# Two blocks on one core: the gaps of a gated scan's level move into the operands' buffer, and the modulation's transposes to another place

## The reference

```python
def hgrn_forget(z, lb):
    f = lb + (1.0 - lb) * jax.nn.sigmoid(z)
    return 1.0 - f, jnp.log(f)                      # key, log of the forget gate

def step(s, xs):                                    # gla_chunk_scan
    bcum = jnp.cumsum(fc, axis=1)
    o_inter = einsum('bthk,bhkv->bthv', qf * jnp.exp(bcum), s)
    diff = bcum[:, :, None] - bcum[:, None, :]
    decay = jnp.exp(jnp.where(incl, diff, -inf))
    att = einsum('bthk,bshk,btshk->bhts', qf, kf, decay)
    o_intra = einsum('bhts,bshv->bthv', att, vf)
    ...
```

## Time and profile before

| | |
|---|---|
| median of three runs | 1472.39 us |
| the profiled execution | 1471.23 us |
| its span | 1469.5 us |
| TensorE matmuls, busy | 1411.3 us (96%) |
| TensorE weight loads, busy | 1155.2 us (79%) |
| VectorE, busy | 563.9 us (38%) |
| ScalarE, busy | 415.0 us (28%) |
| GpSimd, busy | 157.2 us (11%) |

### The profile page before, as it was taken

The page is one execution under the profiler, slowest core; times in us unless marked ns, Lnnn a source line. Parts: engine busy times, 40 slices in busy tenths (PEclk is TensorE's granted clock), DMA queues, the critical chain, the costliest instruction groups (busy, mean ns, idle before and its releaser), DMA issues.

```text
span 1469.5 us, 20226 instructions
## 1 busy us (share of the span) xinstructions
PE 1411.3 (96%) x8130; PEld 1155.2 (79%) x8130; DVE 563.9 (38%) x1335; ACT 415.0 (28%) x771; POOL 157.2 (11%) x191
## 2 busy tenths in 40 slices
PE   5999999999999999999999999999979999999986
PEld 3888788888878888888888888877757788887765
DVE  1262322111226432313235431245664533466363
ACT  2112212412011222333323312331333422433432
POOL 0110300000011030000111100003230000142100
PEclk9999999999999999999999999999989999999998
DMA  9544544355445444443333332455313433322200
GB/s 388 218 163 152 206 172 172 134 200 194 184 164 211 175 173 172 149 179 117 141 126 132 115 127 103 144 200 201 116 58 144 172 119 147 126 112 87 87 29 29
DMA packets 31485, 221.76 MB, mean 151 GB/s; under 512 B 3872, under 2 KB 4000, under 8 KB 4896
## 3 DMA queue, kind: packets, MB, share of 16 engines
q1 hardware_dynamic: 31392, 220.47, 40.5%
HBM read 219.41 MB, written 1.05 MB: 150 GB/s over the span
## 4 chain that ended last, share of the span: by engine, by line
PE 84%; DVE 7%; ACT 2%; issue 2%; POOL 2%; DMA 1%; DVEq 0%; SPq 0%; ACTq 0%; POOLq 0%
PE event L879 43%; PE event L870 9%; PE event L1023 6%; PE event L1067 5%; PE logits L955 3%; PE mixed_out L1011 3%; PE event L836 3%; PE event L1035 2%; PE turns L974 2%; PE event L1167 2%; PE event L1094 1%; DMA ring<-in_w 1%; PE event L1048 1%; DVE logits L1612 1%; ACT S L1284 1%
## 5 line engine op out<-in xcount | busy, mean ns | idle before, releaser
L879 PE MATMUL event<-u,ring 128*128 128x256 f32 x3200 | 717.7, 383 | 15.3 <-ACT region L1233 9.5
L879 PEld LDWEIGHTS event<-u,ring 128*128 128x128 f32 x3200 | 605.7, 191 | 113.0 <-issue 30.9
L870 PE MATMUL event<-ring,u 128*128 128x256 f32 (+1 forms) x704 | 150.9, 371 | 0.0
L870 PEld LDWEIGHTS event<-ring,u 128*128 128x128 f32 x704 | 127.4, 190 | 20.9 <-issue 4.9
L1975 POOL TENSOR_TENSOR raw<-raw,tables 128x512 f32<-128x512 f32 (+1 forms) x28 | 44.7, 1595 | 758.3 <-DVE turned L1588 449.5
L1248 ACT ACTIVATE region<-event 128x512 f32<-128x512 f32 x72 | 43.0, 597 | 279.9 <-PE event L879 279.7
L1284 ACT ACTIVATE S<-logits,stat 128x512 f32<-128x512 f32 (+2 forms) x160 | 83.8, 535 | 127.8 <-DVE stat L1627 123.2
L1067 PE MATMUL event<-region,ring 128*128 128x256 f32 x384 | 85.1, 380 | 2.9 <-DVE region L1770 2.9
L1023 PE MATMUL event<-region,ring 128*128 128x256 f32 x384 | 84.4, 380 | 0.0
L1067 PEld LDWEIGHTS event<-region,ring 128*128 128x128 f32 x384 | 72.2, 190 | 15.2 <-issue 5.9
L1023 PEld LDWEIGHTS event<-region,ring 128*128 128x128 f32 x384 | 72.6, 190 | 11.1 <-issue 1.4
(11 more groups left out here) (208 smaller groups left out, 1307.5 us busy)
## 6 DMA issues: line engine op xcount, KB each, us to landing
ring<-in_w SPq DMA_DIRECT2D x204, 1024.0 KB, 4.8
tables<-in_two SPq DMA_DIRECT2D x1, 1472.0 KB, 8.0
x<-in_x SPq DMA_DIRECT2D x1, 1024.0 KB, 14.8
x<-in_ctx SPq DMA_DIRECT2D x1, 1024.0 KB, 6.7
out<-x SPq DMA_DIRECT2D x4, 256.0 KB, 2.2
tables<-in_one SPq DMA_DIRECT2D x1, 768.0 KB, 9.9
tables<-in_late SPq DMA_DIRECT2D x1, 512.0 KB, 5.6
consts<-in_common SPq DMA_DIRECT2D x1, 320.0 KB, 3.3
```

The lines of the kernel that those rows point to most:

```text
L870: ins = mm(bank[:, t * 256:t * 256 + width], mem.u[:, q, k, t * P:(t + 1) * P], wt[:, k * 256:k * 256 + width], start=k == 0, stop=k == KB ...
L879: ins = mm(bank[:, j * 256:(j + 1) * 256], wt[:, k * 256 + j * P:k * 256 + j * P + P], mem.u[:, q, k, :], start=k == 0, stop=k == KB - 1)
```

## The change

Two edits. In the first, GpSimd writes the gaps of prep p straight into `mem.ops[:, p % 2]`, where ScalarE exponentiates them and VectorE multiplies in place. GpSimd used to wait for the products of prep p-1 (`ops_ready`); it now waits until TensorE has run what reads that slot from prep p-2 (`full` of the events that `readers` gives), if there is such a prep in the section. In the second, `modulate` puts `ada` behind the next heavy item after its `mva`, in place of two items later. An unused function is taken out as well.

```diff
-def modulate(s, at, lag, groups):
+def modulate(s, at, groups):
+
+    after = {a: min(n for n in heavy(s) if n > a) for a in at}
     out = []
     for n, item in enumerate(s):
         out.append(item)
         for (tag, g), a in zip(groups, at):
+            if after[a] == n:
+                out.append(("ada", g, tag))
+        for (tag, g), a in zip(groups, at):
             if a == n:
                 out += group(tag, g)
-            if a + lag == n:
-                out.append(("ada", g, tag))
     return out
@@
-    s = modulate(s, heavy(s)[3::5][:8], 2, groups)
+    s = modulate(s, heavy(s)[3::5][:8], groups)
@@
-    s = modulate(s, heavy(s)[2::4][:6], 2, [("v0", g) for g in range(6)])
+    s = modulate(s, heavy(s)[2::4][:6], [("v0", g) for g in range(6)])
@@
+    def event(self, item):
+
+        e, seen = self.phase, []
+        for i in self.script:
+            i = i[1] if i[0] == "half" else i
+            if i == item:
+                return e
+            if i not in seen:
+                e += self.events(i)
+                seen.append(i)
+
+    def readers(self, s, m):
+
+        if m == "khat":
+            e = self.event(("khatT", s))
+            return [e, e + 1]
+        if m == "qc":
+            return [self.event(("hout", s))]
+        e = self.event(("level", s, m))
+        return [e, e + 1]
@@ scalar
                 p = preps.index(item[1:])
+                ops = mem.ops[:, all_preps.index(item[1:]) % 2]
                 eng.wait_ge(sems["gaps_ready"], w.at("gaps_ready", p + 1))
-                act(mem.gaps, mem.gaps, ACT.Exp).then_inc(sems["decays_ready"], 1)
+                act(ops, ops, ACT.Exp).then_inc(sems["decays_ready"], 1)
@@ vector
                 else:
-                    tt(ops[:, 0], gaps[:, 0], to["hq"], ALU.mult)
+                    tt(ops[:, 0], ops[:, 0], to["hq"], ALU.mult)
                     for side, k in ((0, "ff"), (1, "fb")):
-                        ins = tt(halves_of(ops[:, 1], m)[side], halves_of(gaps[:, 1], m)[side],
+                        ins = tt(halves_of(ops[:, 1], m)[side], halves_of(ops[:, 1], m)[side],
                                  halves_of(to[k], m)[side], ALU.mult)
@@ pool
                 eng.wait_ge(sems["cums_ready"], w.at("cums_ready", decays))
-                at = preps.index((s, m))
-                eng.wait_ge(sems["ops_ready"], w.at("ops_ready", at))
-                gaps, FG = mem.gaps, mem.of[s, layer_of(sec, s)]["FG"]
+                p = preps.index((s, m))
+                if p >= 2:
+                    for ev in sec.readers(*preps[p - 2]):
+                        eng.wait_ge(full[ev % BANKS], w.fills(ev))
+                gaps, FG = mem.ops[:, p % 2], mem.of[s, layer_of(sec, s)]["FG"]
```

More of the change, by code:

```diff
@@ L246, in script_one1 @@
     return s
[L249 to L254, removed]
 def lay(fill, start, stop, items):
@@ L1186, in body @@
         sqs = [i[1] for i in sec.script if i[0] == "sq"]
-        preps = [i[1:] for i in sec.script if i[0] == "prep" and i[2] != 0]
+        all_preps = [i[1:] for i in sec.script if i[0] == "prep"]
+        preps = [p for p in all_preps if p[1] != 0]
         stick = 0
@@ L1847, in body @@
                 p = preps.index((s, m))
-                ops, gaps, to = mem.ops[:, p % 2], mem.gaps, mem.of[s, layer_of(sec, s)]
+                ops, to = mem.ops[:, p % 2], mem.of[s, layer_of(sec, s)]
                 if m == 0:
@@ L1858, in body @@
                 if m == "khat":
-                    tt(ops[:, 0], gaps[:, 0], to["ff"], ALU.mult)
-                    ins = tt(ops[:, 1], gaps[:, 1], to["fb"], ALU.mult)
+                    tt(ops[:, 0], ops[:, 0], to["ff"], ALU.mult)
+                    ins = tt(ops[:, 1], ops[:, 1], to["fb"], ALU.mult)
                 elif m == "qc":
-                    tt(ops[:, 0], gaps[:, 0], to["hq"], ALU.mult)
-                    ins = tt(ops[:, 1], gaps[:, 1], to["hq"], ALU.mult)
+                    tt(ops[:, 0], ops[:, 0], to["hq"], ALU.mult)
+                    ins = tt(ops[:, 1], ops[:, 1], to["hq"], ALU.mult)
                 else:
-                    tt(ops[:, 0], gaps[:, 0], to["hq"], ALU.mult)
+                    tt(ops[:, 0], ops[:, 0], to["hq"], ALU.mult)
                     for side, k in ((0, "ff"), (1, "fb")):
-                        ins = tt(halves_of(ops[:, 1], m)[side], halves_of(gaps[:, 1], m)[side],
+                        ins = tt(halves_of(ops[:, 1], m)[side], halves_of(ops[:, 1], m)[side],
                                  halves_of(to[k], m)[side], ALU.mult)
```

## The result

The kernel after takes 1476.93 us in the median of six runs (1475.85 to 1480.69), the kernel before 1471.04 (1470.36 to 1472.88). The ratio is 1.0041, with a 95% interval from 1.0030 to 1.0052: 5.9 us slower, where 1477.5 us was predicted. The profiled execution of after is the slowest of its six, 1480.69 us with a span of 1479.0. So I don't read its end time but how far each level starts behind the same level of before, and what was lost between them.

The account below looks back on a forecast made before the run. TensorE, busy 1411.3 of 1469.5 us, was taken to bound the kernel. Scan +4.9 (1.2 + 1.1 + 2.1 + 0.5) and modulation +0.4 made +5.3, giving 1477.5 us from the three-run median 1472.39; range 1472.0 to 1483.5.

Parts of the forecast that it names:

- The 4.1 us in line: Scan preps: after level p-2 ends, gaps and exponential take 4.1 us until products p can start.
- Context scan, +1.2: Prep 16, ahead of the merge: lateness 2.4 us against slack 1.3 makes TensorE wait, +1.2 us.
- rival 3: All scans: every late step costs TensorE its lateness, +25 us, 1498 us; chance 0.02.
- Layer 0, +1.1: Layer 0's latent scan: products 8 come 2.5 us late, less 0.9 and 0.5, delaying the long wait's end by 1.1 us.
- The gained link: Layer 0's scan: gaps 64 no longer wait for products 32 and follow gaps 32 at once, gaining 0.9 us.
- Layer 1, +2.1: Layer 1's latent scan: products 8 come 2.5 us late, less 0.4 for work no longer overlapping gaps, +2.1 us.
- Clock, +0.5: TensorE behind new waits: a third of one half-clock stretch of some 1.5 us, +0.5 us, ends 0 and 3.
- Loss one: Modulation: w1's group 5 leaves the wait between last merge and out 0, costing +0.6 us.
- Loss two: Modulation: v0's group 3 runs behind block av 0, 3.9 to 5.4 us late against slack 3.4, delaying logits 5, +1.2 us.
- Rival 1: Scan lateness is made good before TensorE: scan +0 to +2, sum about 0, 1472.5 us; chance 0.22.
- Rival 2: Layer 0: gaps 64 start 2.7 us sooner, long wait shrinks by up to 2.7, total -3.5, 1469 us; chance 0.07.
- Rival 4: Dearer chain: half clock after two waits (+3) and both modulation losses at their ends, 1481 to 1484 us; chance 0.09.

Follow-up runs that it names:

- own_three: Kernel after, but context prep 16 and both latent scans' preps 8 keep the separate gap tile and old wait: 1471.12 us, ratio 0.9990.
- late_three: Kernel before, but only context prep 16 and both latent scans' preps 8 write gaps into the operands' buffer: 1477.69 us, ratio 1.0044.
- ctx_longer: Kernel after, with each context scan level's first subtraction issued five times: 1483.60 us, ratio 1.0085 to the kernel before.
- edit 1 alone: Kernel after, with modulate and its two calls as before: 1478.12 us, ratio 1.0041 to the kernel before.
- own_all_but_64: Kernel after, but all gap preps save layer 0's 64 keep the separate tile and old wait: 1470.89 us, ratio 0.9990.
- edit 2 alone: Kernel before, with the new modulate: 1471.92 us, ratio 1.0000 to the kernel before.

## Why the prediction was right, point by point

**What bounds it.** As said: TensorE's work is unchanged, and the loss is idle time at three places.

**The 4.1 us in line.** Right. Products were predicted 2.4 to 2.5 us late at the three steps and are 2.60, 2.63 and 2.63 late. Khat's were predicted 1.1 late and are 1.2. The other levels of the context scan are 2.2 to 2.6 late, where 1.9 to 2.4 was predicted. GpSimd's first gap of prep 8 starts 0.23 us behind level 2's matmuls, not 0.1.

**Context scan, +1.2.** The wait is 1.20; the levels behind come 1.46 later. The slack was put at 1.3 and is 1.4, by two different latenesses. The context's other steps cost nothing (own_three), as rival 3's counterargument said.

**Layer 0, +1.1.** 1.35, but by luck. The bare lateness without a link, 2.58 (late_three), is what I had as 2.5. The gained link and the softmax scaling without gaps beside it were put at 0.9 and 0.5 together, 1.4; they are worth 0.5, because the gaps that start earlier run beside VectorE's products and slow them by 0.84. That makes 2.06, as in ctx_longer. The other 0.7 came from the half clock at level 16, which the executions of the kernel after and of edit 1 alone have and ctx_longer and late_three have not. Which of the two is usual the unprofiled runs don't say. I had not counted that TensorE also waits 0.5 us longer for the copy-out ahead of level 2 (1.7 in the waits above, 1.2 before), nor that a wait ahead of the stage's first level is 0.4 shorter; these two cancel.

**Layer 1, +2.1.** 2.73: the term was mis-sized, for the same reason. The credit of 0.4 for work that no longer runs beside GpSimd is not there. Gaps 16 now start at 1324.33, as soon as gaps 8 are done, and run beside products 8, whose pair takes 1.61 us in place of 0.75 (the earlier trace rows have 420 ns for one). A collision that was removed at one place came back at another.

**The rule on GpSimd and VectorE.** VectorE's pair of products took 0.75 us alone and 1.59 to 1.61 beside GpSimd's subtractions, which is the contention that the Trainium skill (GPSIMD Engine Reference, section 1, Specifications) states for VectorE instructions with two SBUF inputs. The trace agrees in kind. As a forecast for the time it would have misled: VectorE's busy time fell by 10.6 us, and the kernel became 5.9 us slower. In own_three VectorE is busy for 555.8 us and in own_all_but_64 for 561.4, and their medians are 1471.12 and 1470.89.

**Clock, +0.5.** Not borne out. Of the four profiled executions with a wait of 2.6 us at layer 1, one has half clock behind it, for 1.7 us, which alone would be +0.4 in the mean. But these four have no half clock at the end, behind the wait of 2.13 us, where four of the other six have one:

```profile
1456.44 5.38 PE L1167 MATMUL event<-u,consts 128*128 128x256 f32 x16 [2.13 <-ACT u L1361]
```

(the kernel before; 3.69 us at full clock). Over all executions the mean granted clock is 0.9905 for edit 1 alone against 0.9899 for the kernel before beside it, and 0.9900 for late_three against 0.9897; the kernel after has 0.9903. It is not lower where the time is longer: the loss is not clock.

**Edit 2, +0.4.** The runs say -0.2, the trace -0.4. The gain was put at 1.4 and is 1.2. Loss one was put at 0.6 and is 0.4. Loss two, 1.2 us, is absent: the lateness was put at 3.9 to 5.4 us against a slack of 3.4, and is 3.3. The step that failed here is the lower end, for which I let VectorE's small instructions become at most 1.5 us faster without GpSimd; they and the scalings won 2.1. A loss of 0.4 ahead of logits 0 was missed: I had named that group's new place and not asked what cover it left.

**The rivals.** Rival 1 (hidden) falls with the three waits. Rival 2's mechanism is real and worth 0.5 to 0.6. Rival 3 falls with own_three. Rival 4's time is reached in the profiled execution of after, 1480.69 us, in which the clock fell twice more, at 1360 and 1411 us, but not in the median; its losses of modulation are not there.

The sum predicted for the scan was +4.9; edit 1 alone is +6.0. Modulation was put at +0.4 and is -0.2. So the total came out at 5.9 against 5.3 with two errors of opposite sign, of 1.1 and 0.6. The time was helped by luck once more: 1477.5 was reckoned from a median of 1472.39 over three runs, which is 1471.04 over six. That base was 1.4 too high and the difference put on it 0.8 too low.

## What to carry to other kernels

When an edit makes a step late on an engine off the critical path, the sum of the lateness says nothing: here 53 us of new waiting cost 6, all of it at three of 28 steps. For each late step follow the queues behind it to the next thing TensorE needs, and compare lateness with slack; one short slack (1.4 us) or one chain without any decides. To save a buffer by letting two stages share it is to put their work in line, so keep the separate buffer at the steps whose slack is smaller than that line, and at those alone. A small item of TensorE that stands in a wait for another engine is free there; moved out of it, it costs its own time (here 0.4 us each, twice).

## What the runs showed of the hardware

- Behind the same wait the granted clock differs from one execution to the next. The wait of 2.35 us ahead of 413 us is in all ten profiled executions; in eight the clock behind it fell to half (1.2 GHz in place of 2.4), in two (edit 2 alone, ctx_longer) it did not. After the 2.6 us at layer 1 it fell in one execution of four, after the 2.4 us at level 16 of layer 0 in two of four, and after the 2.13 us near the end in four of ten. Shorter waits were nearly always followed by full clock, but once it fell behind 1.55 us (late_three, 893 us) and once behind 1.38 us (the kernel after, 1411 us). After the 4.03 us of the context scan TensorE's 16 matmuls took 6.13 us; at full clock 64 of them take 14.08, 3.5 for 16.
- A stretch at half clock ahead of a longer wait cost nothing here and even gave 0.7 us back: level 16 of layer 0 in the kernel after took 2.08 us in place of 1.16, level 32 came 1.5 us later, and so GpSimd's gaps 128 kept out of the way of VectorE's scalings on which the long wait hangs.
- Two 128x256 products on VectorE with two SBUF inputs each take 0.75 us alone and 1.59 us beside GpSimd's 128x256 subtractions. These suffer less: at worst 0.94 to 0.97 us in place of 0.62.
- The start of the kernel differs by several microseconds from one execution to the next: a single wait for the weights of the prologue's modulation, around 22 to 26 us, was 2.4 to 5.4 us long in the ten traces. That is as large as the effects looked for, so the comparison of level starts behind it settles terms of some tenths that the medians can't.
